# Hybrid encoder layer with a mixture of experts: experts ordered by their place in the group, and the expert rows gathered back at two times

## The reference

```python
    g_top, g_idx = lax.top_k(p_group, 1)
    e_top, e_idx = lax.top_k(jax.nn.softmax(e_sel, axis=-1), TOP_K)   # e_sel: the 4 logits of that group
    ...
    for e in range(N_EXPERTS):
        he = jax.nn.silu(t @ w1[e]) * (t @ w3[e])
        y = y + gates[:, e:e + 1] * (he @ w2[e]).astype(jnp.float32)
```

## Time and profile before

| | |
|---|---|
| median of 3 runs | 1319.01 us (1317.9 to 1325.2) |
| profiled execution | 1328.77 us, its span 1327.0 us |
| mean granted TensorE clock | 0.927 |
| busy, share of the span | TensorE 84%, VectorE 55%, ScalarE 39%, GpSimd 28% |
| expert slots in the trace | `Silu` of slot 0 at 927.5 us, of slot 31 at 1264.6 us |
| closing stage | first gather at 1276.3 us, last scaled row finished at 1323.7 us |

### The profile page before, as it was taken

The page is one execution under the profiler, slowest core; times in us unless marked ns, Lnnn a source line. Parts: engine busy times, 40 slices in busy tenths (PEclk is TensorE's granted clock), DMA queues, the critical chain, the costliest instruction groups (busy, mean ns, idle before and its releaser), DMA issues.

```text
span 1327.0 us, 18397 instructions
## 1 busy us (share of the span) xinstructions
PE 1113.3 (84%) x5855; PEld 895.7 (67%) x5855; DVE 733.5 (55%) x1336; ACT 520.5 (39%) x935; POOL 370.2 (28%) x370
## 2 busy tenths in 40 slices
PE   3999999969976889899899999954898988988920
PEld 3889899945564777677777776743676767777720
DVE  3430510156665566556464654437786877787837
ACT  4333222123332222222222322304776777777712
POOL 2100500001053111101010101103665656656556
PEclk9999999979987989899989998975999999999975
DMA  6340141152058566574535452904788786764576
GB/s 244 109 148 0 57 132 47 46 128 65 7 206 297 199 207 214 183 252 145 191 143 190 144 175 89 329 34 150 265 270 297 253 276 231 256 224 180 186 266 233
DMA packets 104596, 234.44 MB, mean 177 GB/s; under 512 B 15104, under 2 KB 63696, under 8 KB 95312
## 3 DMA queue, kind: packets, MB, share of 16 engines
q1 hardware_dynamic: 81264, 117.68, 26.0%
q0 software_dynamic: 22176, 113.78, 24.6%
q10 hardware_dynamic: 1088, 2.10, 0.5%
HBM read 234.92 MB, written 48.94 MB: 214 GB/s over the span
## 4 chain that ended last, share of the span: by engine, by line
PE 54%; DVE 11%; DMA 10%; issue 10%; ACT 8%; POOL 4%; SPq 2%; POOLq 1%; ACTq 0%; DVEq 0%
DMA below<-in_w 6%; PE ps L1013 4%; PE ps L903 4%; PE ps L2060 4%; PE ps L2062 4%; PE ps L2061 4%; PE ps L885 3%; DVE low L1737 3%; PE ps L972 3%; ACT high L1452 3%; PE ps L1054 3%; PE ps L1055 2%; PE ps L1056 2%; PE ps L2055 2%; PE ps L2054 2%
## 5 line engine op out<-in xcount | busy, mean ns | idle before, releaser
L1737 DVE TENSOR_TENSOR low<-below,high 128x1024 fp32r<-128x1024 f32 x128 | 193.7, 1560 | 75.2 <-ACT high L1452 65.6
L1415 POOL TENSOR_TENSOR low<-below,high 128x1024 fp32r<-128x1024 f32 x64 | 146.4, 2305 | 108.1 <-ACT high L1473 108.1
L1550 PE MATMUL ps<-high 128*128 128x512 f32 x384 | 156.2, 407 | 15.7 <-DVE low L1747 11.4
L1552 PE MATMUL ps<-high,low 128*128 128x512 f32 x384 | 151.4, 394 | 0.0
L1551 PE MATMUL ps<-low,high 128*128 128x512 f32 x384 | 151.2, 394 | 0.0
L1452 ACT ACTIVATE high<-below 128x1024 fp32r<-128x1024 f32 x128 | 129.5, 1052 | 43.6 <-DMA below<-in_w 43.0
L618 ACT ACTIVATE arena<-ps 128x512 f32<-128x512 f32 (+8 forms) x100 | 51.7, 527 | 201.4 <-PE ps L885 200.9
L885 PE MATMUL ps<-arena 128*128 128x128 f32 (+4 forms) x613 | 96.9, 283 | 12.5 <-ACT arena L865 4.4
L1918 POOL TENSOR_SCALAR arena<-arena 128x1 f32<-128x1 f32 (+5 forms) x38 | 14.0, 367 | 306.1 <-ACT arena L843 131.3
L1550 PEld LDWEIGHTS ps<-high 128*128 128x128 f32 x384 | 73.0, 190 | 36.3 <-issue 19.0
L769 POOL DMA_DIRECT2D high<-wo_dram x30 | 16.4, 547 | 284.7 <-PE ps L1056 268.2
(11 more groups left out here) (228 smaller groups left out, 2290.6 us busy)
## 6 DMA issues: line engine op xcount, KB each, us to landing
below<-in_w SPq DMA_DIRECT2D x256, 256.0 KB
high<-wo_dram POOLq DMA_DIRECT2D x32, 1024.0 KB, 5.3
low<-wo_dram POOLq DMA_DIRECT2D x32, 1024.0 KB, 7.4
below<-in_w POOLq DMA_DIRECT2D x64, 512.0 KB
y_dram<-arena SPq DMA_DIRECT2D x32, 512.0 KB, 3.1
arena<-in_x_prompt SPq DMA_DIRECT2D x16, 512.0 KB
below<-in_w_in SPq DMA_DIRECT2D x12, 512.0 KB, 6.7
out<-arena SPq DMA_DIRECT2D x9, 512.0 KB, 4.5
```

The costliest lines, as they stand in the source:

```text
L1415: pool.tensor_tensor(w2_lo[s % UN][:, c], w2_in[:, c], w2_hi[s % UN][:, c].bitcast(F32), ALU.subtract).then_inc(s_w2lo, 1)
L1550: pe.matmul(out, x_hi, w_hi, start=start, stop=False)
L1552: return pe.matmul(out, x_lo, w_hi, start=False, stop=stop)
L1737: dve.tensor_tensor(chunk(w13_lo[j], c), chunk(w13_in, c), chunk(w13_hi[j], c).bitcast(F32), ALU.subtract).then_inc(s_w13lo, 1)
```

## The change

- The experts are laid out in the order place in the group, then group. The host permutes `w1`, `w2` and `w3` to match. A token's two experts are in one group at different places, so the one with the lower place is among the first 12 experts, and its slot is below 128 * `EARLY`, `EARLY` = 28, for any routing.
- `order_pairs` (VectorE, in slot 0) sorts each token's two slots and gates: index 0 is the lower slot.
- The gathers of the first rows (`ya`) are issued by GpSimd in slots 30 and 31, tile by tile with two buffers; a buffer is free when the tile two before has been added. VectorE adds them (`first_adds`) at the end of slot 30 (tiles 0, 1), at the start of slot 31 (2 to 4), after slot 31's `g_lo` (5) and after the last half row (6 to 8). Only then comes the barrier.
- All nine loads of `res` are issued by SyncE in slot 28.
- After the barrier GpSimd issues the nine gathers of the second rows (`yb`) in a row, then takes the nine roots. VectorE does one add per tile, and `finish` comes three tiles behind the adds.
- Slots 28 and 29 are written out rather than run in the loop.

```diff
+EARLY = (2 * sum(MOE_ROWS) + (P - 1) * (NE - NG)) // P
...
-    AHEAD = 5
-    RES_LATE = len(res)
+    LAG = 3
+    old = Region(hg_base)
+    res.append(old.take(D))
+    ya = old.take(2, D)
...
@@ expert_turns
-        with eng.Fori(2, turns) as it:
+        with eng.Fori(2, turns - 1) as it:
             for j in range(UN):
                 body(it, j, False, False)
-        for j in range(UN):
-            body(turns, j, False, j == UN - 1)
+        for it in (turns - 1, turns):
+            for j in range(UN):
+                body(it, j, False, it == turns and j == UN - 1)
@@ moe_loads
+            if isinstance(s, int) and s == EARLY:
+                sp.wait_ge(s_h1st, 16 * NT)
+                sp.wait_ge(s_slots, 2)
+                for t in range(NT):
+                    load_res(t)
...
-        sp.wait_ge(s_h1st, 16 * NT)
-        for t in range(RES_LATE):
-            load_res(t)
@@ moe_pool
+        def fetch(k, t, to):
+
+            pool.indirect_dma_start(
+                out=to[0:MOE_ROWS[t]], out_offset=None, in_=y_dram[0:SLOTS if k else EARLY * P],
+                in_offset=bass.IndirectOffsetOnAxis(ap=slot_i[0:MOE_ROWS[t], k, t:t + 1], axis=0)
+                ).then_inc(s_yab[t], 16)
+
+        def fetch_first(tiles):
+
+            for t in tiles:
+                if t == 0:
+                    pool.wait_ge(s_slots, 2)
+                    for j in range(UN):
+                        pool.wait_ge(s_yst[j], 16 * len(range(j, EARLY, UN)))
+                if t >= 2:
+                    pool.wait_ge(s_comb, t - 1)
+                fetch(0, t, ya[:, t % 2, :])
...
+            if s == SLOT_TILES - 2:
+                fetch_first(range(2))
+        fetch_first(range(2, NT))
         end_phase(pool, 2)
...
-        for t in range(AHEAD):
-            fetch(t)
+        for t in range(NT):
+            fetch(1, t, yb[:, t, :])
         for t in range(NT):
             R = MOE_ROWS[t]
             rsqrt_mean(y_stat[0:R, 1, t:t + 1], y_stat[0:R, 0, t:t + 1], D, s_ysq, s_yrs, t + 1)
-            if t + AHEAD < NT:
-                fetch(t + AHEAD)
@@ moe_dve
-        def expert_row(k, oh, order="p (t g j) -> p t g j"):
+        def expert_row(k, oh, order="p (t j g) -> p t g j"):
...
+        def order_pairs():
+
+            one, two = rt[:, 10, 0:NT], rt[:, 10, NT:2 * NT]
+            first, a, b = (rt[:, 11, k * NT:(k + 1) * NT] for k in range(3))
+            dve.tensor_tensor(rt[:, 9, 0:NT], one, two, ALU.min)
+            dve.tensor_tensor(rt[:, 9, NT:2 * NT], one, two, ALU.max)
+            link(dve.tensor_tensor(first, one, two, ALU.is_lt))
...
+        def first_adds(tiles):
+
+            for t in tiles:
+                R = MOE_ROWS[t]
+                if t == 0:
+                    dve.wait_ge(s_slots, 2)
+                    dve.wait_ge(s_res, 16 * NT)
+                dve.wait_ge(s_yab[t], 16)
+                dve.scalar_tensor_tensor(out=res[t][0:R, :], in0=ya[0:R, t % 2, :], scalar=gates[0:R, 0, t:t + 1],
+                                         in1=res[t][0:R, :], op0=ALU.mult, op1=ALU.add).then_inc(s_comb, 1)
...
             if not last:
                 split_weights(s + 1, (j + 1) % UN)
+            else:
+                first_adds(range(2, 5))
             dve.wait_ge(s_ms, s + 1)
...
+            if isinstance(s, int) and s == SLOT_TILES - 2:
+                first_adds(range(2))
 
         expert_turns(dve, body)
+        first_adds(range(5, 6))
         free_last(dve)
         y_half(SLOT_TILES - 1, (SLOT_TILES - 1) % UN)
+        first_adds(range(6, NT))
         end_phase(dve, 2)
...
-            link(dve.scalar_tensor_tensor(out=x, in0=ya[0:R, t, :], scalar=gates[0:R, 0, t:t + 1], in1=x,
-                                          op0=ALU.mult, op1=ALU.add))
-            dve.scalar_tensor_tensor(out=x, in0=yb[0:R, t, :], scalar=gates[0:R, 1, t:t + 1], in1=x,
-                                     op0=ALU.mult, op1=ALU.add).then_inc(s_comb, 1)
-            if t:
-                finish(t - 1)
-        finish(NT - 1)
+            dve.scalar_tensor_tensor(out=res[t][0:R, :], in0=yb[0:R, t, :], scalar=gates[0:R, 1, t:t + 1],
+                                     in1=res[t][0:R, :], op0=ALU.mult, op1=ALU.add).then_inc(s_comb, 1)
+            if t >= LAG:
+                finish(t - LAG)
+        for t in range(NT - LAG, NT):
+            finish(t)
@@ host
+        if name in ("w1", "w2", "w3"):
+            a = np.ascontiguousarray(a.reshape(1, NG, EG, *a.shape[2:]).swapaxes(1, 2).reshape(a.shape))
```

34 lines of the change are left out of this document (17 added, 17 removed).

## The result

The changed kernel took 1333.24 us (median of 20 runs, 1323.14 to 1343.78), the kernel before 1324.78 (20 runs beside them, 1317.90 to 1330.04). The ratio is 1.0052 with a 95% interval of [1.0032, 1.0071]: 6.9 us slower, between 4.2 and 9.4. It leaves out the one run of 1343.78 us, which fell into a slower state of the chip. The forecast was 1320.4 us and no change, the range ended at 1329. The profiled execution took 1333.16 us with a span of 1331.4, against 1327.0 before.

A forecast was written before the change was run, and what follows sets the result against it. It took GpSimd's queue to bound the closing stage, while TensorE was busy 10.2 of 11 us in trailing slots. Slot 31's +17.1 less the closing stage's 15.7 gave +1.4 on 1319.0: 1320.4 us, range 1309 to 1329.

The forecast's parts named there:

- slot 31 pays back what the closing stage gains: Main forecast: first closing gather 17.1 us later, closing stage 15.7 us shorter, so no measurable change; chance 0.53.
- the base of the sum: Median of three runs of the kernel before, 1319.0 us, to which the predicted change was added.
- Barrier 0.45 us and first gather: After the last first-row add at 1292.6: the barrier, then the first closing gather (S) at 1293.4, against 1276.3 before.
- The closing stage: From the first closing gather (S) to the last `finish`: 31.7 us instead of 47.4, bounds 29.5 and 36.
- the hidden adds: First-row adds of tiles 0 and 1, taken to fit from 1260.7 to 1263.6 in VectorE's idle 4.84 us before `g_row`.
- The small parts: `res` loads in slot 28 (0, up to 3 us), `order_pairs` in slot 0 (0, under 5 us), and the experts' order.
- The order of the experts: Across the slots: same numbers of each kind of slot in both orders, so 0, with 2 us allowed either way.
- One of the prediction's own signs of being wrong: The prediction is wrong if slots 0 to 30 move by more than 3 us.
- Slow gathers: Rival: landings of tiles 2, 4 and 8 take 7.0 us each, 7.2 us more in all, 1327.6 us; chance 0.22.
- the adds fit into the idle time: Rival: slot 31's `g_row` at most 2 us late, 10 us faster, 1309 us; chance 0.2 including a partial form.
- the Trainium skill's fit for a GpSimd-issued DMA: 2.0 us plus bytes over 436e3, 3.2 us for 512 KB; short landings would make the sum -2.8 us, 1316.2.
- The Trainium skill's rule on the shared SBUF interface: GpSimd and VectorE contend on two-input instructions; every closing gather during adds would be slow, ending at S + 36.

The follow-up runs named there:

- e9: The changed kernel with GpSimd no longer reporting at the third barrier, the others waiting for three; ratio to the kernel before 1.0050 [1.0023, 1.0078].
- e4: The changed kernel with first rows of tiles 2 to 7 gathered into free weight staging and adds placed later; ratio to the kernel before 0.9971 [0.9946, 0.9995].
- e6: e5 with each root issued between the gathers, root t behind the gather of tile t + 5; ratio to the kernel before 0.9973 [0.9945, 1.0000].
- e11: e10 with the roots in four groups and `finish` five tiles behind the add; ratio to the kernel before 0.9925 [0.9898, 0.9953].
- e1: The kernel before with only the new order of the experts; ratio to the kernel before 0.9983 [0.9960, 1.0005].
- e2: The changed kernel with the old order of the experts; ratio to the kernel before 1.0027 [1.0004, 1.0049].
- e12: e11 without the gathers of the first rows of tiles 4 to 8, so part of the work is missing; ratio to the kernel before 0.9900 [0.9863, 0.9936].
- e5: e4 with VectorE reporting at the barrier ahead of the adds of tiles 5 to 8; ratio to the kernel before 0.9960 [0.9936, 0.9983].
- e10: e5 without GpSimd's report at the third barrier, second gathers from tile 5 waiting for their first row's add; ratio to the kernel before 0.9968 [0.9939, 0.9998].

## Why the prediction was wrong

The mechanism was right for the most part: slot 31 pays back what the closing stage gains. What failed are sizes and one wait. The largest was the base of the sum, 5.8 us. Of the mechanism, the term "Barrier 0.45 us and first gather" failed: what stood there was GpSimd's drain, 1.8 us more. The closing stage was taken 1.3 us too short.

**The median it stood on.** 1319.0 was the median of three runs; over 20 runs it is 1324.8. Of the 12.8 us between forecast and result this is 5.8. The remaining 7.1 are the difference between the kernels, 8.5 by the medians, less the +1.4 forecast. The text named the spread of the three runs and did not widen the range by it. On the median of 20 runs the forecast would have been 1326.2 us and the range would have ended at 1334.8, with the result in it.

**Slot 31, step by step.** The clocks of the two traces differ here by 0.1 us, so the prediction's times can be laid beside the rows:

| step | predicted | measured |
|---|---|---|
| adds of tiles 0 and 1 done | 1263.6 | 1266.1 |
| gather of tile 2 starts | 1264.2 | 1265.2 |
| add of tile 2 starts | 1268.8 | 1270.6 |
| `g_row` | 1276.5 | 1277.6 |
| last product starts | 1279.0 | 1279.7 |
| half row 31 done | 1285.0 | 1284.9 |
| last add starts, ends | 1291.2, 1292.6 | 1291.0, 1292.3 |
| S | 1293.4 | 1295.0 |

Up to the last add the chain came as described, order and waits alike, but that each time fits so well is luck in part, since errors cancelled: 2.5 us late with the hidden adds, 1 to 1.8 us after that, and won back where the last product took 4.4 us and not 5.2, as its matmuls were back at 0.23 us apart after the first seven, at 0.37 to 0.57. **The term that failed is "Barrier 0.45 us and first gather".** From the end of the last add to S 0.8 us was forecast and it was 2.6, as the barrier waited for GpSimd's drain. e9 prices this at 1.65 us of S in the changed kernel, and in e4 to e6 the drain ends some 9 us behind the last of five gathers. The two hidden adds were mis-sized too: 2.09 and 2.58 us beside GpSimd's subtraction, where 1.28 was taken. They stayed hidden, since the gather of tile 2 waited for the subtraction.

**The closing stage**, 33.0 us where 31.7 was forecast. The first root let `finish` start at S + 13.8 and not 13.1; the passes ran at 1.2 us as predicted; the four last `finish` waited for roots of 2.0 us and not 1.6, which is 0.9 us. In e11, with grouped roots, the last six follow each other without a wait.

**The small parts.** The nine loads of `res` and the small operations on VectorE left slots 26 to 31 at 52.8 us against 52.7, so taking 0 for the loads was right; `order_pairs`, in slot 0, is not priced by any run. The order of the experts was given 0 with 2 us either way; e1 and e2 neither confirm nor exclude that. One of the prediction's own signs of being wrong did come: from `Silu` of slot 0 to that of slot 31 it took 337.1 us before and 340.9 after, 3.7 more where 3 was the limit. The scatter of that stretch between traces is wider than this limit, so the sign says little.

**What followed from the sum.** The two places make +4.2 us, the two spans differ by 4.4, and the timed difference is 6.9 [4.2, 9.4]. The agreement of the spans is luck in part, as 3.6 us less ahead of slot 0 stand against 3.6 us more in slots 0 to 26. So the mechanism accounts for the lower end of the interval. Whether the rest, up to 2.7 us by its middle, is scatter or a small effect of the order of the experts stays open.

**The rivals.** Slow gathers had the right sign and the wrong mechanism: the trips of tiles 2, 4 and 8, from the start of the gather to the start of the add, took 5.4, 4.3 and 4.7 us, and not 7.0. That the adds fit into the idle time fell in the form in which it was meant; e4 shows that it lacked buffers, and is still only 3.8 us faster where this rival had 10. The range missed because the scatter of the three runs was not in it; GpSimd's drain was not in it either, but with its 1.65 us alone in the sum the result would still have been outside. The rows of the prediction did not hold that drain, but the trace that they came from did, 7.23 and 8.37 us long, and hidden or outside the stage that was being priced. On the Trainium skill's fit for a GpSimd-issued DMA (DMA: Bandwidth & Descriptors, Anatomy of one DMA), which gave 3.2 us: no landing of `L1414` in the changed kernel was under 4.2 us, so the row was the better price. The Trainium skill's rule on the shared SBUF interface (GPSIMD Engine Reference, 1. Specifications) held where the adds ran beside GpSimd's subtraction: the adds took 2.09 and 2.58 us, and the subtraction 4.94 us instead of 3.95. Of the nine gathers in the closing stage only two took 1.87 us and the others 0.9 to 1.0, which is far from the full price of that rule.

## What to carry to other kernels

Work that moves from a closing stage into an earlier one takes its buffers along: with two buffers, nine transfers of 4 to 5 us are a chain of five round trips, whatever idle time lies around them, so count round trips before idle microseconds. Where GpSimd reports at a barrier, price its drain, look in the trace before for how long its drains take even where they cost nothing, and look at who reports there. When a wait is taken away, read who releases the same instruction next: here it was buffers, then the drain, then a store that shared the DMA engines. And read the end of the kernel too, since a wait left out in one place can come back in another, as the drain did in e9. Last, a forecast of half a per cent needs a base that is known to better than that.

## What the runs showed of the hardware, beyond what was expected

- GpSimd's drain behind indirect gathers ended 3.0 to 3.1 us after the last row had landed in seven traces (changed kernel: landed at 1291.0, drain ended at 1294.1), which is 6.1 us after the issue of a single gather and 9.0 to 9.3 after five.
- With no gather on its way it was as long in some places and short in others: 7.2 us at the second barrier of every kernel, 7.4 to 8.3 at the end of e9 to e12, and 1.4 to 2.1 at the first barrier and at the end of the other ten. The long ones stand behind plain loads that GpSimd had issued since its previous drain (80 issues before the second barrier, 64 in the slots), the short ones behind none. That the loads are the reason is not shown, as no run leaves them out.
- A two-input pass of VectorE over 128x1024 took 1.28 us alone and 2.09 to 2.58 us beside GpSimd's subtraction; in e4, e5 and e11 two of them took 6.4 to 6.5 us together, beside the subtraction and a gather's issue.
- The store of one row of slots, 512 KB, let the first gather go 3.7 us behind its half row on a quiet queue and 8.1 us (e11) or 5.5 us (e10) with five gathers, four of them of the same size, beside it.
- GpSimd's operations on one column took 0.19 and 0.57 us with VectorE idle, 1.28 and 0.55 or 0.75 and 1.47 us with VectorE busy. On four columns they took 0.23 and 2.04 us and on three 1.17 and 1.78 (e11), so a group costs little more than one root.
- Behind the same pause of 1.7 to 1.9 us the last product ran at 0.23 us a matmul in e4 and e11 and fell to 0.43 for seven or eight of its twelve in e6 and e10. What decided it no run shows.
